# Pool mixing of a hybrid decoder layer: plain fp32 matmuls replaced by three fp32r matmuls of high and low parts

## The chip, the cores and the metric

The kernel runs on one core of one Trainium2 chip. Its five engines each work through a queue of their own: TensorE (PE in the profile; PEld is its weight load), VectorE (DVE), ScalarE (ACT), GpSimd (POOL) and SyncE (SP, which here only starts transfers). They wait for each other by semaphores. The metric is the device time of one execution, in microseconds (us); less is better.

## The reference

One decoder layer over 256 tokens of width 2048. A normalised input goes through one combined projection of twelve column groups of 512; three branches read it: causal attention of 8 heads, a pooling mixer of 4 groups of 128 channels, and cross-attention of 4 heads into 256 memory tokens. Each is gated, all are concatenated, projected out, added to the input and normalised. The change is in the pooling mixer:

```
outs = []
for g, w in enumerate(POOL_WINDOWS):                  # 2, 4, 8, 16
    csg = cs[..., g*128:(g+1)*128]                    # running sum of u
    prev = jnp.pad(csg, ((0, 0), (w, 0), (0, 0)))[:, :S]
    outs.append((csg - prev) / cnt)                   # trailing-window mean
pooled = jnp.stack(outs, axis=2) - uf                 # mean minus token
mixed = jnp.einsum('bsgc,gcd->bsgd', pooled, w_pool)  # four 128x128 maps
y_p = mixed * pool_scale * silu(g_p)
```

## The kernel before

The projections run in fp32r, which takes a matmul in one pass but keeps fewer bits than fp32. So every operand X is split into a high part (a copy rounded to fp32r) and a low part (X minus the high part), and a product is made of high x high, high x low and low x high.

**Units.** The weights come in pieces of 128 x 1024 numbers (two slices of 128 rows by 512 columns). A group of 512 columns (MK, MV, Q0, ..., U, GA0, GA1, GP, QM, GM, then the output groups) is eight units, a = 0 to 7. For unit n, SP loads the piece, ACT writes its high part `w_hi` (L916), DVE its low part `w_lo` (L1167), and PE multiplies (L660 by the high part, 512 columns: high and low part of the activations side by side; L663 by the low part, 256 columns). Four units' halves fit (`SPLIT = 4`): in the code of step n ACT and DVE split unit n + 4. ACT may overwrite a half when PE has used the unit before it (`piece_used`); PE waits for the low part of its unit (`lo_done`).

**Order.** The order of each engine is that of the code: a loop over the units, in which the other work is put behind conditions such as `g == GP and a == 3`. Nothing overtakes on an engine. In a step, ACT and DVE first split unit n + 4 and then do most of the step's other work; PE first multiplies its unit. So DVE's step a is not tied in time to PE's step a; it can lie before or behind it.

**The pooling.** `window_sums` and `window_means` on DVE make `u_pad[:, :, PAD:]` (4 blocks of 128 channels x 256 tokens), the second of them in steps 3 and 4 of GA1 (L1370 to L1372), and count `pooled_ready` up to 4. The maps `wp` (128 x 4 x 128) are loaded early by SP. In group GP, behind its unit a = 5, PE waits for both and multiplies (L879). ACT, in its own step GP 5, waits for `mixed`, scales the four results (L1103) and hands them to the gate.

**What else is in group GP.** ACT and DVE also split the memory keys there (`mk_hi` L1081 in ACT's step 1, `mk_lo` in DVE's step 2) and the memory values (`mv_hi` L1084 in ACT's step 3, `mv_lo` in DVE's step 4; both low parts by the helper at L1341), finish the gate of the group before (DVE L1454 in step 1, behind POOL's product L611), and split it (ACT L1114 in step 1, DVE L1459 in step 2). Their users come much later, with the group GM.

At the start of the kernel PE runs eleven matmuls of ones (L807), which compute nothing that is used.

The lines of PE that the change replaces:

```
if g == GP and a == 5:
    pe.wait_ge(wp_landed, 16)
    pe.wait_ge(pooled_ready, NF)
    for i in range(NF):
        m = pe.matmul(ps[:, bank0(g + 1) + i, 0:S], wp[:, i, :], u_pad[:, i, PAD:], ...)
    m.then_inc(mixed, 1)
```

Of the kernel before, what the change touches and what calls it, by code (L numbers as in the profile page):

```python
# [22 lines left out]
F32R = mybir.dt.float32r  # L23
ALU = mybir.AluOpType
ACT = mybir.ActivationFunctionType
AX = mybir.AxisListType

P = 128
D = 2048
S = 256  # L30
# [4 lines left out]
NF = COLS // P  # L35
# [4 lines left out]
PAD = WINDOWS[-1] // 2  # L40
# [77 lines left out]
def build(nc, x, mem, x_t, mem_head, columns, w_in, w_mem_kv, w_pool, w_out, final_g, out):  # L118
    with ExitStack() as ctx:
        def sb(name, shape, dt=F32, stack=ctx):  # L120
            return stack.enter_context(nc.sbuf_tensor(name, shape, dt))

        def sem(name):
            return ctx.enter_context(nc.semaphore(name))
# [7 lines left out]
        early = ExitStack()  # L132
        xT = sb("xT", [P, KT, 2, S], F32R, early)
        early.close()
        early = ExitStack()
# [4 lines left out]
        early = ExitStack()  # L140
# [3 lines left out]
        early = ExitStack()  # L144
        sb("y_of_branches", [P, (KT - NF) * 2 * S], F32, early)
        u_pad = sb("u_pad", [P, NF, PAD + S], F32, early)
        early.close()
        early = ExitStack()
        mem_rows = sb("mem_rows", [P, TH, D], F32, early)
        early.close()  # L150
        early = ExitStack()
# [5 lines left out]
        early = ExitStack()  # L157
# [3 lines left out]
        early = ExitStack()  # L161
# [43 lines left out]
        sum_b = sb("sum_b", [P, NF, PAD + S], F32, early)  # L205
        early.close()
        early = ExitStack()
        xs_hi = sb("xs_hi", [P, BLOCKS, 4, TPP, P], F32R, early)
        xs_lo = sb("xs_lo", [P, BLOCKS, 4, TPP, P], F32R, early)
        early.close()  # L210
# [97 lines left out]
        u_ready = sem("u_ready")  # L308
        pads_zero = sem("pads_zero")
        pooled_ready = sem("pooled_ready")  # L310
        mixed = sem("mixed")
        gate_tanh = sem("gate_tanh")
        gate_att = sem("gate_att")
# [41 lines left out]
        def bank0(g):  # L355

            return BANK.get(g, 4 * (g % 2))
# [271 lines left out]
        def _(pe):  # L629
# [199 lines left out]
            for n in range(PAIR):  # L829
                g, a = unit(n)  # L830

                if n == K_PAIR:
                    pe.wait_ge(evacuated, Q0 + 1)
                if n == V_PAIR:
                    pe.wait_ge(evacuated, Q1 + 1)
                if in_pair(n):
                    unit_of_pair(n)
                    if n == K_TURNED:
                        turn_keys()
                    continue  # L840
                if a == 0 and g >= 2:
                    pe.wait_ge(evacuated, g - 1)
                if a == 0 and g == U:
                    pe.wait_ge(kT_ready, 2)
                if a == 0 and g - 1 in BRANCHES:
                    pe.wait_ge(att_ready, 2 * (BRANCHES.index(g - 1) + 1))
                if n < HIGH_FIRST:
                    high_parts_first(n)
                    continue
                if g == MK:  # L850
                    pe.wait_ge(mem_lo, TPP * (a + 1))
                if g == Q0:
                    pe.wait_ge(x_lo, a + 1)
                if g == OUT0 and a % 2 == 0:
                    pe.wait_ge(y_lo, a // 2 + 1)
                pe.wait_ge(lo_done, n + 1)
                if g == OUT0:
                    rows_are_tokens(n, yT).then_inc(piece_used, 1)
                elif g in TOKENS_ON_ROWS:
                    rows_are_tokens(n, memT if g == MV else xT).then_inc(piece_used, 1)  # L860
                else:
                    rows_are_features(n, memT if g == MK else xT)

                if g in JOBS:
                    if a == int(g == MEM_JOB):
                        pe.wait_ge(evacuated, g)
                        scores(g, 0)
                        scores(g, 1)
                    if a == 4 + int(g == GA0):
                        turn_probs(g, 0)  # L870
                        turn_probs(g, 1)
                    if a == 6:
                        weigh_values(g, 0)
                        weigh_values(g, 1)
                if g == GP and a == 5:
                    pe.wait_ge(wp_landed, 16)
                    pe.wait_ge(pooled_ready, NF)
                    for i in range(NF):
                        m = pe.matmul(ps[:, bank0(g + 1) + i, 0:S], wp[:, i, :], u_pad[:, i, PAD:], start=True, stop=True)  # L879
                    m.then_inc(mixed, 1)  # L880

            pe.wait_ge(evacuated, OUT0)
# [15 lines left out]
        def _(act):  # L898
# [124 lines left out]
            for n in range(PAIR):  # L1023
# [55 lines left out]
                if g == GP and a == 1:  # L1079
                    act.wait_ge(mk_scaled, 1)  # L1080
                    act.activation(mk_hi[:, :, :], mkT[:, :, :], ACT.Copy).then_inc(mk_hi_done, 1)  # L1081
                if g == GP and a == 3:
                    act.wait_ge(mv_scaled, 1)
                    act.activation(mv_hi[:, :, :], mv[:, :, :], ACT.Copy).then_inc(mv_hi_done, 1)  # L1084
# [70 lines left out]
        def _(dve):  # L1155
# [183 lines left out]
            def low(lo, whole, hi):  # L1339

                return dve.tensor_tensor(lo[:, :, :], whole[:, :, :], hi[:, :, :].bitcast(F32), ALU.subtract)  # L1341
# [41 lines left out]
            for n in range(PAIR):  # L1383
# [47 lines left out]
                if g == GP and a == 2:  # L1431
                    dve.wait_ge(mk_hi_done, 1)
                    low(mk_lo, mkT, mk_hi).then_inc(mk_split, 1)
                if g == GP and a == 4:
                    dve.wait_ge(mv_hi_done, 1)
                    low(mv_lo, mv, mv_hi).then_inc(mv_split, 1)
# [145 lines left out]
```

## Time and profile before

| | us |
|---|---|
| median of 3 runs | 428.13 |
| lowest and highest of them | 428.09, 428.76 |
| the profiled execution's own time | 428.26 |
| its span in the profile | 426.5 |
| PE busy | 417.3 |
| DVE busy | 313.6 |
| ACT busy | 249.5 |
| POOL busy | 43.4 |

The span runs from the first to the last instruction that the profile shows; 1.76 us of the execution's time lie around it. Busy times are sums over the whole span. A duration of a matmul in the profile includes the time it spends in PE's pipeline, in which the next ones are already running: the distance from one start to the next is what a matmul costs in a stream of them. The same holds, by less, for DVE and ACT.

### The profile page before, as it was taken

The numbers are of one execution on the slowest core, as the hardware profiler recorded it, in microseconds if no ns is written. First come the engines' busy times: TensorE is split into PE (matmuls) and PEld (weight loads), VectorE is DVE, ScalarE is ACT, GpSimd is POOL, SyncE is SP. The second block draws the span as 40 slices with busy tenths as digits, with TensorE's granted clock in tenths as the row PEclk, the third lists the DMA queues.
The fourth block names the chain that finished last, engine by engine and source line by source line (L and its number), as shares of the span: only waits on it lengthen the run. The fifth ranks groups of instructions, "written<-read, shape, count | busy, mean of one in ns | idle before, by whom it ended". The sixth has DMA issues, their size and how long they took to land.

```text
span 426.5 us, 5775 instructions
## 1 busy us (share of the span) xinstructions
PE 417.3 (98%) x2184; PEld 357.9 (84%) x2184; DVE 313.6 (74%) x342; ACT 249.5 (58%) x335; POOL 43.4 (10%) x68
## 2 busy tenths in 40 slices
PE   8999999999999999999999999999999999999993
PEld 7888888888888888888888888888899888888882
DVE  4876888477987896856566778887667488897853
ACT  6764785257665667368465444755565566665611
POOL 1000003101001000000000341401000301000160
PEclk9999999999999999999999999999999999999998
DMA  8999739999599378955398256565646999467023
GB/s 285 415 414 421 315 105 303 297 412 320 146 386 271 129 25 328 421 226 197 100 116 243 62 184 202 192 199 167 228 148 223 247 405 275 186 246 295 3 87 110
DMA packets 29115, 99.48 MB, mean 233 GB/s; under 512 B 3872, under 2 KB 4384, under 8 KB 28192
## 3 DMA queue, kind: packets, MB, share of 16 engines
q1 hardware_dynamic: 24912, 84.31, 57.3%
q0 software_dynamic: 1728, 6.29, 8.0%
q10 hardware_dynamic: 2448, 8.52, 5.3%
q8 instruction: 17, 0.28, 0.3%
q14 instruction: 10, 0.08, 0.0%
HBM read 97.01 MB, written 2.10 MB: 232 GB/s over the span
## 4 chain that ended last, share of the span: by engine, by line
PE 91%; issue 3%; DVE 3%; DMA 1%; ACT 1%; DVEq 0%; POOLq 0%; POOL 0%; ACTq 0%
PE ps L660 29%; PE ps L663 14%; PE ps L719 4%; PE ps L717 4%; PE ps L718 4%; PE ps L676 4%; PE ps L678 4%; PE ps L677 4%; PE ps L702 4%; PE ps L700 4%; PE ps L701 4%; PE ps L641 3%; PE ps L648 1%; DMA mem_raw<-in_mem_head 1%; DVE x_f L1178 1%
## 5 line engine op out<-in xcount | busy, mean ns | idle before, releaser
L1167 DVE TENSOR_TENSOR w_lo<-w_raw,w_hi 128x1024 fp32r<-128x1024 f32 x131 | 163.3, 1263 | 61.5 <-ACT w_hi L916 60.6
L916 ACT ACTIVATE w_hi<-w_raw 128x1024 fp32r<-128x1024 f32 x131 | 135.9, 1056 | 64.7 <-PE ps L663 27.7
L660 PE MATMUL ps<-xT,w_hi 128*128 128x512 f32 x512 | 161.7, 397 | 0.0
L663 PEld LDWEIGHTS ps<-xT,w_lo 128*128 128x128 f32 x512 | 96.2, 188 | 22.7
L663 PE MATMUL ps<-xT,w_lo 128*128 128x256 f32 x512 | 100.6, 278 | 0.0
L660 PEld LDWEIGHTS ps<-xT,w_hi 128*128 128x128 f32 x512 | 78.3, 189 | 0.3
L717 PE MATMUL ps<-w_hi,xT 128*128 128x512 f32 x64 | 24.9, 389 | 0.0
L718 PE MATMUL ps<-w_lo,xT 128*128 128x512 f32 x64 | 24.9, 389 | 0.0
L719 PE MATMUL ps<-w_hi,xT 128*128 128x512 f32 x64 | 24.9, 389 | 0.0
L916 ACT ACTIVATE w_hi<-x_f 128x1024 fp32r<-128x1024 f32 x14 | 14.8, 1059 | 15.5 <-PE ps L719 10.1
L1167 DVE TENSOR_TENSOR w_lo<-x_f,w_hi 128x1024 fp32r<-128x1024 f32 x14 | 17.1, 1224 | 6.4 <-ACT w_hi L916 6.3
L1058 ACT ACTIVATE part_b<-ps 128x1024 f32<-128x1024 f32 x9 | 9.2, 1024 | 15.1 <-PE ps L663 15.1
L676 PE MATMUL ps<-w_hi,yT 128*128 128x512 f32 x46 | 17.9, 389 | 0.0
L677 PE MATMUL ps<-w_lo,yT 128*128 128x512 f32 x46 | 17.9, 389 | 0.0
L678 PE MATMUL ps<-w_hi,yT 128*128 128x512 f32 x46 | 17.9, 389 | 0.0
L718 PEld LDWEIGHTS ps<-w_lo,xT 128*128 128x128 f32 x64 | 12.0, 188 | 2.5
L717 PEld LDWEIGHTS ps<-w_hi,xT 128*128 128x128 f32 x64 | 12.0, 188 | 2.5
L719 PEld LDWEIGHTS ps<-w_hi,xT 128*128 128x128 f32 x64 | 12.0, 188 | 2.5
L641 PE MATMUL ps<-memT,w_hi 128*128 128x512 f32 x48 | 13.2, 396 | 0.7 <-DVE memT L1265 0.7
L611 POOL TENSOR_TENSOR gate<-gate,att 128x1024 f32<-128x1024 f32 x4 | 9.6, 2411 | 37.3 <-ACT part_b L1109 37.3
L1114 ACT ACTIVATE yT<-gate 128x1024 fp32r<-128x1024 f32 x4 | 4.2, 1062 | 15.0 <-DVE gate L1454 15.0
L621 POOL TENSOR_TENSOR x_res<-x_res,fg 128x512 f32<-128x512 f32 x6 | 8.0, 1365 | 49.0 <-DVE w_lo L1167 49.0
(220 smaller groups left out, 699.3 us busy)
## 6 DMA issues: line engine op xcount, KB each, us to landing
w_raw<-in_w_in SPq DMA_DIRECT2D x92, 512.0 KB, 6.7
w_raw<-in_w_out SPq DMA_DIRECT2D x30, 512.0 KB, 5.0
w_raw<-in_w_mem_kv SPq DMA_DIRECT2D x13, 512.0 KB, 12.2
x_f<-in_w_in SPq DMA_DIRECT2D x6, 512.0 KB, 7.1
x_f<-in_w_in POOLq DMA_DIRECT2D x6, 512.0 KB, 9.4
x_t_raw<-in_x_t SPq DMA_DIRECT2D x8, 256.0 KB, 12.9
rows<-in_x ACTq DMA_DIRECT2D x2, 1024.0 KB, 10.1
mem_rows<-in_mem ACTq DMA_DIRECT2D x2, 1024.0 KB, 10.2
```

The lines of the kernel that those rows point to most:

```text
L641: pe.matmul(ps[:, bank0(MK) + f, :], hi[:, t, f * P:(f + 1) * P], memT[:, kt], start=(kt == 0), stop=False, skip_group_check=True)
L660: pe.matmul(ps[:, bank0(g) + f, :], hi[:, t, f * P:(f + 1) * P], moving[:, kt], start=(kt == 0), stop=(kt == KT - 1), skip_group_check=True)
L663: m = pe.matmul(ps[:, bank0(g) + f, 0:S], lo[:, t, f * P:(f + 1) * P], moving[:, kt, 0], start=False, stop=(kt == KT - 1), skip_group_chec ...
L676: pe.matmul(acc, stationary[:, kt, 0, tok], hi[:, t, :], start=(kt == 0), stop=False)
L677: pe.matmul(acc, stationary[:, kt, 0, tok], lo[:, t, :], start=False, stop=False)
L678: m = pe.matmul(acc, stationary[:, kt, 1, tok], hi[:, t, :], start=False, stop=(kt == last))
L700: pe.matmul(ps[:, bank, :], left[0], hi[:, t, :], start=not begun, stop=False, skip_group_check=True)
L717: pe.matmul(acc, rows[:, kt, 0, tok], hi[:, t, :], start=not begun, stop=False, skip_group_check=True)
L718: pe.matmul(acc, rows[:, kt, 0, tok], lo[:, t, :], start=False, stop=False, skip_group_check=True)
L719: m = pe.matmul(acc, rows[:, kt, 1, tok], hi[:, t, :], start=False, stop=end_of, skip_group_check=True)
L916: act.activation(halves_of(n)[0], whole_of(n), ACT.Copy).then_inc(hi_done, 1)
L1167: dve.tensor_tensor(lo, whole_of(n), hi.bitcast(F32), ALU.subtract).then_inc(lo_done, 1)
```

## The change

PE's wait in GP 5 is now for a new semaphore `pool_split` (two counts), and each of the four fp32 matmuls is three fp32r matmuls of the same output size, into the same place. ACT writes the high parts of the maps and of the pooled values in its step GP 2, and DVE the low parts in its step GP 3. The four new tensors lie in the place that `sum_a` and `sum_b` share with others; that place doesn't grow.

```
@@ tensors
+        pooled_hi = sb("pooled_hi", [P, NF, S], F32R, early)
+        pooled_lo = sb("pooled_lo", [P, NF, S], F32R, early)
+        wp_hi = sb("wp_hi", [P, NF, P], F32R, early)
+        wp_lo = sb("wp_lo", [P, NF, P], F32R, early)
@@ PE, group GP, behind unit 5
-                    pe.wait_ge(wp_landed, 16)
-                    pe.wait_ge(pooled_ready, NF)
+                    pe.wait_ge(pool_split, 2)
                     for i in range(NF):
-                        m = pe.matmul(ps[:, bank0(g + 1) + i, 0:S], wp[:, i, :], u_pad[:, i, PAD:], start=True, stop=True)
+                        acc = ps[:, bank0(g + 1) + i, 0:S]
+                        pe.matmul(acc, wp_hi[:, i, :], pooled_hi[:, i, :], start=True, stop=False)
+                        pe.matmul(acc, wp_hi[:, i, :], pooled_lo[:, i, :], start=False, stop=False)
+                        m = pe.matmul(acc, wp_lo[:, i, :], pooled_hi[:, i, :], start=False, stop=True)
                     m.then_inc(mixed, 1)
@@ ACT
+                if g == GP and a == 2:
+                    act.wait_ge(wp_landed, 16)
+                    act.wait_ge(pooled_ready, NF)
+                    act.activation(wp_hi[:, :, :], wp[:, :, :], ACT.Copy).then_inc(pool_hi_done, 1)
+                    act.activation(pooled_hi[:, :, :], u_pad[:, :, PAD:], ACT.Copy).then_inc(pool_hi_done, 1)
@@ DVE
+                if g == GP and a == 3:
+                    dve.wait_ge(pool_hi_done, 2)
+                    low(wp_lo, wp, wp_hi).then_inc(pool_split, 1)
+                    low(pooled_lo, u_pad[:, :, PAD:], pooled_hi).then_inc(pool_split, 1)
```

How the rows stand on the engines, from units GP 4 to GM 2. In DVE's queue before, from the low part of unit GP 6 on (the L1167 rows are, in this order, GP 6, then GP 7 and GM 0, then GM 1 and GM 2):

```order
L1167 TENSOR_TENSOR w_lo<-w_raw,w_hi 128x1024 [waits hi_done]
L1341 TENSOR_TENSOR mk_lo<-mkT,mk_hi 128x1024 [waits mk_hi_done]
L1459 TENSOR_TENSOR yT<-gate,yT 128x4x256 [waits y_hi]
L1167 TENSOR_TENSOR w_lo<-w_raw,w_hi 128x1024 [waits hi_done] x2
L1341 TENSOR_TENSOR mv_lo<-mv,mv_hi 128x1024 [waits mv_hi_done]
L1167 TENSOR_TENSOR w_lo<-w_raw,w_hi 128x1024 [waits hi_done] x2
```

The same place after the change (L1182 is what L1167 was, L1356 what L1341 was):

```order
L1182 TENSOR_TENSOR w_lo<-w_raw,w_hi 128x1024 [waits hi_done]
L1356 TENSOR_TENSOR mk_lo<-mkT,mk_hi 128x1024 [waits mk_hi_done]
L1478 TENSOR_TENSOR yT<-gate,yT 128x4x256 [waits y_hi]
L1182 TENSOR_TENSOR w_lo<-w_raw,w_hi 128x1024 [waits hi_done]
L1356 TENSOR_TENSOR wp_lo<-wp,wp_hi 128x512 [waits pool_hi_done]
L1356 TENSOR_TENSOR pooled_lo<-u_pad,pooled_hi 128x1024
L1182 TENSOR_TENSOR w_lo<-w_raw,w_hi 128x1024 [waits hi_done]
L1356 TENSOR_TENSOR mv_lo<-mv,mv_hi 128x1024 [waits mv_hi_done]
L1182 TENSOR_TENSOR w_lo<-w_raw,w_hi 128x1024 [waits hi_done] x2
```

The two new low parts stand between the low parts of units GP 7 and GM 0. In ACT's queue after the change, from the split of the gate on (L926 was L916; its rows are the high parts of units GP 6, GP 7, GM 0, GM 1):

```order
L1129 ACTIVATE yT<-gate 128x4x256 [waits y_ready]
L926 ACTIVATE w_hi<-w_raw 128x1024 [waits landed2,piece_used]
L1095 ACTIVATE wp_hi<-wp 128x512 [waits pooled_ready,wp_landed]
L1096 ACTIVATE pooled_hi<-u_pad 128x1024
L926 ACTIVATE w_hi<-w_raw 128x1024 [waits landed3,piece_used]
L1099 ACTIVATE mv_hi<-mv 128x1024 [waits mv_scaled]
L926 ACTIVATE w_hi<-w_raw 128x1024 [waits landed4,piece_used]
L926 ACTIVATE w_hi<-w_raw 128x1024 [waits landed5,piece_used]
L1118 ACTIVATE att<-ps,cols 128x256 [waits y_ready,mixed]
```

The two new high parts stand between those of units GP 6 and GP 7. Nothing else has moved on any engine.

## Rows read from the trace of the kernel before

**Rows 1.** The page: busy times with shares of the span, and the chain's shares.

```profile
PE 417.3 (98%) x2184; PEld 357.9 (84%) x2184; DVE 313.6 (74%) x342; ACT 249.5 (58%) x335; POOL 43.4 (10%) x68
...
PE 91%; issue 3%; DVE 3%; DMA 1%; ACT 1%; DVEq 0%; POOLq 0%; POOL 0%; ACTq 0%
```

**Rows 2.** All waits of PE (what, for what: us in total, times, longest).

```profile
PE ps L807 <- POOL ones L546: 1.0, 1, 1.0
PE ps L641 <- DVE memT L1265: 0.7, 1, 0.7
```

**Rows 3.** Timeline of PE at the pool's mixing (start us, length us).

```profile
274.85 0.40 PE L663 MATMUL ps<-xT,w_lo 128*128 128x256 f32 x2
275.08 1.89 PE L879 MATMUL ps<-u_pad,wp 128*128 128x256 f32 x8
```

**Rows 4.** The chain of waits, same place (start us, length us).

```profile
275.24 1.73 PE ps L879 x8
```

**Rows 5.** Timeline of DVE, the units of group GP ([idle before <- releaser]).

```profile
273.14 1.23 DVE L1167 TENSOR_TENSOR w_lo<-w_raw,w_hi 128x1024 fp32r<-128x1024 f32 x1 [2.08 <-ACT w_hi L916]
274.29 1.76 DVE L1341 TENSOR_TENSOR mk_lo<-mkT,mk_hi 128x1024 fp32r<-128x1024 f32 x1
275.98 1.21 DVE L1459 TENSOR_TENSOR yT<-gate,yT 128x1024 fp32r<-128x1024 f32 x1
277.11 2.35 DVE L1167 TENSOR_TENSOR w_lo<-w_raw,w_hi 128x1024 fp32r<-128x1024 f32 x2
279.38 1.21 DVE L1341 TENSOR_TENSOR mv_lo<-mv,mv_hi 128x1024 fp32r<-128x1024 f32 x1
```

**Rows 6.** Timeline of PE: scores with the memory, first of 24, and what follows the last.

```profile
310.24 0.28 PE L746 MATMUL ps<-mk_hi,qm_hi 128*128 128x256 f32 x1
...
313.11 0.63 PE L660 MATMUL ps<-xT,w_hi 128*128 128x512 f32 x2
```

**Rows 7.** Timeline of ACT, same stretch.

```profile
271.10 1.07 ACT L1114 ACTIVATE yT<-gate 128x1024 fp32r<-128x1024 f32 x1 [3.04 <-DVE gate L1454]
272.07 1.99 ACT L916 ACTIVATE w_hi<-w_raw 128x1024 fp32r<-128x1024 f32 x2
```

**Rows 8.** Splits of 128x512, by line (duration ns min/median/max).

```profile
L1255 DVE TENSOR_TENSOR w_lo<-w_raw,w_hi x3: 685/687/692, 5.7 to 10.0; 128x512 fp32r<-128x512 f32 x3
...
L922 ACT ACTIVATE w_hi<-w_raw x3: 612/617/632, 5.0 to 9.1; 128x512 fp32r<-128x512 f32 x3
```

**Rows 9.** Timeline: PE after its wait for DVE at the start.

```profile
5.27 0.48 DVE L1265 SCALAR_TENSOR_TENSOR memT<-mem_raw,memT 128x256 fp32r<-128x256 f32 x1 [5.27 <-ACT memT L941]
...
5.81 1.20 PE L641 MATMUL ps<-memT,w_hi 128*128 128x512 f32 x4 [0.69 <-DVE memT L1265]
...
7.32 1.09 PE L641 MATMUL ps<-memT,w_hi 128*128 128x512 f32 x4
```

**Rows 10.** Timeline of POOL around it.

```profile
273.37 1.61 POOL L601 TENSOR_TENSOR s_raw<-gate,s_raw 128x256 f32<-128x256 f32 x1
287.42 2.42 POOL L611 TENSOR_TENSOR gate<-gate,att 128x1024 f32<-128x1024 f32 x1 [12.45 <-ACT part_b L1109]
```

**Rows 11.** PE's last matmul; windows after it (the third number from the end: granted clock).

```profile
418.78 0.28 PE L733 MATMUL ps<-w_hi,yT 128*128 128x256 f32 x1
...
423.50:424.00 0.50, 0.00 (x0) 0.00 (x0) 0.00 (x0) 0.00 (x0) 0.00 (x0) 0.80 1.25 393
424.00:425.00 1.00, 0.00 (x0) 0.00 (x0) 0.00 (x0) 0.00 (x0) 0.00 (x0) 0.50 0.98 336
```

**Rows 12.** PE's first matmuls: by line, then the timeline of two short windows.

```profile
L807 PE MATMUL ps<-ones x22: 275/421/583, 1.0 to 4.8; 128*128 128x128 f32 x22
...
1.01 1.23 PE L807 MATMUL ps<-ones 128*128 128x128 f32 x4 [1.01 <-POOL ones L546]
...
4.29 0.83 PE L807 MATMUL ps<-ones 128*128 128x128 f32 x6
```

More of the change, by code:

```diff
@@ L207, in build @@
         early = ExitStack()
+        pooled_hi = sb("pooled_hi", [P, NF, S], F32R, early)
+        pooled_lo = sb("pooled_lo", [P, NF, S], F32R, early)
+        wp_hi = sb("wp_hi", [P, NF, P], F32R, early)
+        wp_lo = sb("wp_lo", [P, NF, P], F32R, early)
+        early.close()
+        early = ExitStack()
         xs_hi = sb("xs_hi", [P, BLOCKS, 4, TPP, P], F32R, early)
@@ L310, in build @@
         pooled_ready = sem("pooled_ready")
+        pool_hi_done = sem("pool_hi_done")
+        pool_split = sem("pool_split")
         mixed = sem("mixed")
```

## The prediction, as it was put on record

> **What bounds the kernel now.** Read the page's busy times first: PE is busy for 98% of the span, and the chain that ended last runs through PE for 91% of it [rows 1]. Then PE's waits: in the whole execution it waits twice, 1.0 and 0.7 us, both in the first 6 us [rows 2]. So PE is the bound everywhere, a time taken off its stream comes off the end, and a time for which PE is made to wait goes onto the end, as long as no later wait of PE is there to take it up; there is none. The other engines matter only where they come too late for PE.
>
> Then read the place of the change. The eight passes of the four fp32 matmuls start at 275.08, directly behind the last matmul of unit GP 5 [rows 3], and hold PE for 1.73 us on the chain, 0.216 each [rows 4]. PE doesn't wait for the pooled values there, since they are done long before: it waits for nothing.
>
> Last, read DVE's timeline beside it, since PE is to wait for DVE now. A unit takes PE about 2.8 us, and DVE's queue is a fixed order. While PE ends GP 5 at 275.08, DVE has just begun `mk_lo` (274.29), which belongs to its own step GP 2 [rows 5]. DVE prepares units four ahead, so PE isn't disturbed by that; but other work in DVE's step a = 3 isn't done when PE is at a = 3, it is done when DVE gets there. This offset between the steps of the two engines is what decides the change.
>
> **PE's own work, a gain.** Removed: eight passes, 1.73 us [rows 4]. Added: twelve fp32r matmuls of 128x256. The same shape with the same pattern of high and low parts stands in the scores with the memory: 24 of them take from 310.24 to 313.11, 0.1196 each [rows 6]. 12 x 0.1196 = 1.435 us. The gain is 0.29 us, 0.07% of the whole. The bound on the bad side is the fp32 pass of the old code, 0.216: 12 x 0.216 = 2.59, a loss of 0.86; I take the scores' row, since type, shape and pattern are those of the change.
>
> The Trainium skill ("TensorE: Matmul & The Clock Gate", Back-to-back issue gap) gives a warm matmul of N columns as N/2.4 + 2.5 ns. That is 109 ns for 256 columns, so 1.31 us and a gain of 0.42; the 119.6 ns of the rows decides.
>
> **ACT's new work, hidden.** `wp_hi` and `pooled_hi` come behind the high part of unit GP 6, the first of the two L916 rows at 272.07; the second, GP 7, would follow at about 273.02 [rows 7]. What they wait for is long there. `wp_hi` is 128x512, 0.62 us alone [rows 8], some 0.53 in a row of them; `pooled_hi` is as large as `w_hi`, 0.95 in a row. So both end near 274.6, and the high part of GP 7 ends near 275.6 in place of 274.1. DVE wants that one only at 277.11 [rows 5]; 1.5 us of slack remain. The high parts of GM 0 and GM 1 move by the same 1.5 us and are wanted by DVE after 280. Cost: nothing; without that slack it would be up to 1.5 us on DVE.
>
> **PE's new wait, the loss.** `pool_split` comes from DVE, in this order: low part of GP 6 at 273.14, `mk_lo` at 274.29, the gate's low part at 275.98, the low parts of GP 7 and GM 0 from 277.11 on [rows 5]. The change puts its two subtractions between these last two. Two of them take 2.35, one alone 1.21, so the second starts 1.14 behind the first, at 278.25: there `wp_lo` starts now. It is 128x512, 0.687 long [rows 8], of which about 0.08 overlaps the next, as with the others; `pooled_lo` starts at 278.86 and takes 1.21, like `mv_lo` of the same size [rows 5]: it ends at 280.07. At the start of the kernel PE begins 0.06 us after the end of the DVE row that it waited for (5.27 + 0.48 = 5.75, then 5.81) [rows 9]. So PE begins the mixing at 280.13 and not at 275.08: a stall of 5.05 us. The first matmuls after that earlier wait took 1.20 for four where the next four took 1.09 [rows 9]: 0.1 more for a pipeline that has run empty.
>
> What bounds this term: DVE's rows up to 278.25 are those of before, since nothing ahead of them changes. The two new subtractions could be slowed by POOL, as `mk_lo` looks slowed: 1.76 us, while POOL's L601 runs from 273.37 to 274.98. But POOL has no work from there to 287.42 [rows 10], so I take 1.21; at `mk_lo`'s rate it would be 0.55 more for `pooled_lo` and about 0.3 for `wp_lo`. On the good side, two more starts that overlap better could save 0.1 or 0.2.
>
> **Who else waits.** Behind PE's stalled mixing stand units GP 6, GP 7 and all the rest; nothing overtakes it. ACT goes on meanwhile up to its scaling of the result, which waits for PE, and DVE goes on to the low part of GM 1. When PE comes back they are further ahead of it than before, by the 1.8 us of new DVE work less than the whole stall, so they make PE wait nowhere behind it. The loads from memory are also at least as early relative to PE. No second cost; and no return either, since PE has no later wait to shorten [rows 2]. The tail of the kernel hangs on PE's last matmuls and shifts with them.
>
> **Sum.** +5.05 - 0.29 + 0.1 = +4.86 us. Against the profiled execution's 428.26 this gives 433.1; against the median of 428.13, 433.0. I say 433.1.
>
> **Rival 1: the clock falls in the stall.** PE stands still from 275.24, the end of its last matmul, to 280.13, 4.9 us; nowhere in the trace of before does it do so in the middle. What the clock does then is seen only at the end: the last matmul ends at 419.06, and the granted clock goes from 1.00 to 0.50 (2.4 to 1.2 GHz) in the window from 423.5, whose mean of 0.80 puts the fall at 423.8, 4.7 us after it [rows 11]. That is as long as the stall, so this one fall says neither yes nor no. The price can be read at the kernel's start: the first four passes over the ones take 1.23 in all, the last six 0.83, the single ones 0.583 and 0.275 [rows 12]. So starts are (1.23 - 0.583)/3 = 0.216 apart at first and (0.83 - 0.275)/5 = 0.111 at the end, a half clock and a full one. The 22 start from 1.01 to 4.8: 21 distances of which about 14 are slow, 3.0 us at the half clock, which lose 1.5 us. With that, 433.1 + 1.5 = 434.6; where half as much is lost, 433.9. The bound is a second stretch of that kind, 436.1, for which no row speaks.
>
> The same page of the Trainium skill (HAM oscillation) warns that idle gaps of PE between bursts bring the half clock back, and that each gap pays for it anew; by it this rival, at 434.6, would be the forecast. Rows of before can't decide it, as no such gap is in them.
>
> **Rival 2, on the other side: DVE is in time and the wait costs nothing.** Then the time is 428.26 - 0.29 = 428.0, the same as before within what can be measured. It decides at the point where `pooled_lo` ends before 275.08. DVE would have to be 5 us earlier in its queue. It did stand idle for 2.08 us before 273.14, waiting for ACT's high part of GP 6, and lost 0.55 in `mk_lo` [rows 5]; without both it would still be 2.4 us late, and the change touches neither. Up to a stall of 1.15 us the result would still be "the same". Against it: every row ahead in DVE's queue is there before as after.
>
> **Rival 3: part of the stall is given back.** If after the stall PE's stream ran denser, because it was slowed by something that comes early now, the time would be lower, say 431 to 432. Against it: units before and behind have the same length, and PE waits for nothing.
>
> **How the numbers follow.** About 0.2% (0.86 us) is what a measurement of this kernel can tell from no change. Chances: forecast with the full clock 0.50, 433.1; clock falls 0.42, 433.9 to 434.8; in time 0.03, 428.0; given back 0.03, 431.5; faster by over 0.2%, for which I see no mechanism, 0.02. The range has to hold the first two with their bounds: below, 433.1 less 0.2 of overlap, less 0.13 for the median and less 0.3 for what the starts of the rows leave open, 432.4; above, 434.6 with up to 0.85 of slowed subtractions, of which I leave in half, and a somewhat longer cold stretch, 435.5. Faster 0.02, the same 0.03, slower 0.95.
>
> **What would show it.** PE's waits show a third one, of some 5 us, for DVE's `pooled_lo`; the first new matmul starts near 280.1, the twelve take 1.4 us, the next unit's start is 4.9 us later than before, and everything behind it, PE's last matmul too, is later by the same. DVE's `wp_lo` starts at 278.2 to 278.3. If the clock falls, the granted clock of a window around 280 to 284 is below 1.00 and matmuls there stand twice as far apart. I am wrong if ACT's new work delays the low part of GP 7 beyond 277.11, if the new subtractions are much longer than 1.9 us together, or if PE is found to begin the mixing before DVE's queue has come to it.

## The result, and the profile after

The changed kernel takes 434.41 us (median of 4 runs, 433.88 to 434.70) where the kernel before takes 428.15 (4 runs, 428.09 to 428.76): 1.0139 times as long, 95% interval 1.0127 to 1.0152. It is slower by 6.3 us. Run again later, beside other kernels, it took 435.55 (5 runs, 434.57 to 435.96), 1.0164 (1.0150 to 1.0178). The profiled execution took 434.70, 6.44 more than that of before.

A word on names first: the group behind GP in the kernel's order is QM. The units that the part on the change and the prediction call GM 0, GM 1 and GM 2 are QM 0, QM 1 and QM 2. Only the name was wrong; the rows and the places meant are the right ones.

All waits of PE in the profile after (what, for what: us in total, times, longest), against the two of [rows 2]:

```profile
PE ps L887 <- DVE pooled_lo L1356: 4.6, 1, 4.6
PE ps L815 <- POOL ones L554: 1.0, 1, 1.0
```

There is one large new wait, and it is for `pooled_lo`. The timeline of PE at the mixing, against [rows 3] (columns: start us, length us; L668 and L671 are what L660 and L663 were):

```profile
275.36 0.40 PE L671 MATMUL ps<-xT,w_lo 128*128 128x256 f32 x2
280.35 0.58 PE L887 MATMUL ps<-pooled_hi,wp_hi 128*128 128x256 f32 x1 [4.59 <-DVE pooled_lo L1356]
280.73 0.41 PE L888 MATMUL ps<-pooled_lo,wp_hi 128*128 128x256 f32 x1
280.94 0.41 PE L889 MATMUL ps<-pooled_hi,wp_lo 128*128 128x256 f32 x1
...
283.07 0.80 PE L668 MATMUL ps<-xT,w_hi 128*128 128x512 f32 x2
283.71 0.40 PE L671 MATMUL ps<-xT,w_lo 128*128 128x256 f32 x2
283.95 0.62 PE L668 MATMUL ps<-xT,w_hi 128*128 128x512 f32 x2
```

Two of the L671 matmuls take 0.23 (275.08 less 274.85 in [rows 3]), so PE would have gone on at 275.59; it goes on at 280.35, a stall of 4.76 us. The profile gives 4.59, since it counts from the modelled end of the last matmul. And from there the new matmuls start 0.21 apart, not 0.12 as in [rows 6]. The granted clock says why (windows; the third number from the end):

```profile
280.00:280.50 0.50, 0.15 (x1) 0.15 (x1) 0.50 (x2) 0.00 (x0) 0.00 (x0) 0.53 0.53 180
283.00:284.00 1.00, 1.00 (x7) 0.88 (x6) 0.69 (x1) 0.69 (x2) 0.00 (x0) 0.78 0.91 336
```

A mean of 0.53 over the first half microsecond is a fall from 1.00 to 0.50 at 280.03, and 0.78 over the later one is a rise back at 283.44: 2.4 to 1.2 GHz and back, 3.4 us in all, of which PE works 3.1.

DVE's queue in the same stretch, against [rows 5] (L1182, L1356 and L1478 are what L1167, L1341 and L1459 were):

```profile
274.52 1.77 DVE L1356 TENSOR_TENSOR mk_lo<-mkT,mk_hi 128x1024 fp32r<-128x1024 f32 x1
276.21 1.21 DVE L1478 TENSOR_TENSOR yT<-gate,yT 128x1024 fp32r<-128x1024 f32 x1
277.34 1.21 DVE L1182 TENSOR_TENSOR w_lo<-w_raw,w_hi 128x1024 fp32r<-128x1024 f32 x1
278.48 0.68 DVE L1356 TENSOR_TENSOR wp_lo<-wp,wp_hi 128x512 fp32r<-128x512 f32 x1
279.08 1.21 DVE L1356 TENSOR_TENSOR pooled_lo<-u_pad,pooled_hi 128x1024 fp32r<-128x1024 f32 x1
```

DVE never pauses in it; the low parts are simply last in a line of five. The kernel's splits are at the places and of the lengths that the prediction gave, 0.23 us later, as the rows ahead of them are in this execution.

### The profile page after: what moved, and what is told of

Its sections match the earlier page's. It is cut to its first block, busy times and chain, and to the rows that moved or that the text cites. A ratio compares the mean times of both kernels' runs of the same rounds, so it can differ in the third digit from the quotient of the medians.

```text
span 432.9 us, 5787 instructions
## 1 busy us (share of the span) xinstructions
PE 419.8 (97%) x2188; PEld 360.5 (83%) x2188; DVE 315.3 (73%) x344; ACT 251.1 (58%) x337; POOL 43.4 (10%) x68
## 4 chain that ended last, share of the span: by engine, by line
PE 87%; DVE 6%; issue 3%; ACT 1%; POOL 0%; DVEq 0%; POOLq 0%; ACTq 0%
PE ps L668 26%; PE ps L671 13%; PE ps L727 4%; PE ps L725 4%; PE ps L726 4%; PE ps L684 4%; PE ps L686 4%; PE ps L685 4%; PE ps L710 4%; PE ps L709 4%; PE ps L708 4%; PE ps L649 3%; DVE w_lo L1182 2%; PE ps L656 1%; ACT w_hi L926 1%
## 5 line engine op out<-in xcount | busy, mean ns | idle before, releaser
L1182 DVE TENSOR_TENSOR w_lo<-w_raw,w_hi 128x1024 fp32r<-128x1024 f32 x131 | 163.4, 1262 | 65.2 <-ACT w_hi L926 64.4
L926 ACT ACTIVATE w_hi<-w_raw 128x1024 fp32r<-128x1024 f32 x131 | 136.0, 1056 | 65.0 <-PE ps L671 27.4
L668 PE MATMUL ps<-xT,w_hi 128*128 128x512 f32 x512 | 161.8, 397 | 0.0
L671 PEld LDWEIGHTS ps<-xT,w_lo 128*128 128x128 f32 x512 | 96.2, 188 | 22.6
L671 PE MATMUL ps<-xT,w_lo 128*128 128x256 f32 x512 | 100.6, 278 | 0.0
L668 PEld LDWEIGHTS ps<-xT,w_hi 128*128 128x128 f32 x512 | 78.5, 189 | 0.3
L926 ACT ACTIVATE w_hi<-x_f 128x1024 fp32r<-128x1024 f32 x14 | 14.8, 1059 | 15.7 <-PE ps L727 10.1
L1182 DVE TENSOR_TENSOR w_lo<-x_f,w_hi 128x1024 fp32r<-128x1024 f32 x14 | 17.1, 1223 | 6.8 <-ACT w_hi L926 6.7
```

Source lines behind the costliest of these rows:

```text
L668: pe.matmul(ps[:, bank0(g) + f, :], hi[:, t, f * P:(f + 1) * P], moving[:, kt], start=(kt == 0), stop=(kt == KT - 1), skip_group_check=True)
L671: m = pe.matmul(ps[:, bank0(g) + f, 0:S], lo[:, t, f * P:(f + 1) * P], moving[:, kt, 0], start=False, stop=(kt == KT - 1), skip_group_chec ...
L926: act.activation(halves_of(n)[0], whole_of(n), ACT.Copy).then_inc(hi_done, 1)
L1182: dve.tensor_tensor(lo, whole_of(n), hi.bitcast(F32), ALU.subtract).then_inc(lo_done, 1)
```

## The experiments

Three questions were open: whether the loss is the wait or the added work, what the clock's share is, and whether the gain on PE is real. The table has every further kernel that was run; `before` is the median of the kernel before on the same chip. "Stall" is from the moment at which PE would have gone on to the first matmul of the mixing, in the one profiled execution. The rows with the same number under `before` were run together on one chip, the others on other chips.

| kernel | median us | lowest, highest | before | ratio, 95% interval | stall |
|---|---|---|---|---|---|
| fit | 428.25 | 427.81, 428.81 | 428.22 | 0.9997 (0.9988, 1.0006) | 0 |
| fit_fp32 | 428.32 | 427.99, 429.02 | 428.22 | 1.0003 (0.9994, 1.0012) | 0 |
| warm | 432.95 | 432.48, 433.12 | 428.22 | 1.0109 (1.0093, 1.0124) | 4.48, filled |
| wait_only | 435.22 | 434.30, 436.89 | 428.22 | 1.0153 (1.0137, 1.0169) | 4.63 |
| stall1 | 429.44 | 429.03, 429.94 | 428.26 | 1.0026 (1.0016, 1.0035) | 1.60 |
| stall2 | 430.87 | 430.11, 431.82 | 428.26 | 1.0049 (1.0030, 1.0068) | 2.77 |
| stall3 | 433.40 | 432.10, 433.93 | 428.26 | 1.0104 (1.0083, 1.0125) | 3.86 |
| fit2 | 427.92 | 427.51, 428.55 | 428.26 | 0.9987 (0.9979, 0.9996) | 0 |
| splits_only | 428.37 | 427.95, 428.76 | 428.28 | 1.0000 (0.9990, 1.0009) | 0 |
| after_fp32 | 435.67 | 433.04, 437.42 | 428.28 | 1.0163 (1.0124, 1.0202) | 5.13 |
| after_again | 435.55 | 434.57, 435.96 | 428.28 | 1.0164 (1.0150, 1.0178) | 5.13 |
| fit2_fp32 | 428.58 | 428.14, 429.06 | 428.28 | 1.0006 (0.9996, 1.0015) | 0 |

### wait_only: the wait without the work

```
@@ before.py, PE, group GP, behind unit 5
                     pe.wait_ge(pooled_ready, NF)
+                    pe.wait_ge(lo_done, n + 4)
```

> The kernel before with one wait more and nothing else: at the mixing PE also waits for DVE's low part of the third unit ahead (the first of group QM), which ends at 279.46 in the trace of before. No splits, plain fp32 matmuls. Theory (the wait on DVE's queue is the loss): a stall of 4.4 us, 432.6 to 432.8 with the full clock, 434.2 to 434.6 if it falls (then eight fp32 passes run at the half clock too). Rival (the loss is ACT's and DVE's added work or the new matmuls): 428.2.

A single line turns 428.2 into 435.2. Not one instruction is added to ACT or DVE, and the matmuls are the old ones. PE's waits and its timeline:

```profile
PE ps L880 <- DVE w_lo L1168: 4.5, 1, 4.5
...
275.90 0.40 PE L663 MATMUL ps<-xT,w_lo 128*128 128x256 f32 x2
280.76 3.75 PE L880 MATMUL ps<-u_pad,wp 128*128 128x256 f32 x8 [4.46 <-DVE w_lo L1168]
283.95 1.41 PE L660 MATMUL ps<-xT,w_hi 128*128 128x512 f32 x2
...
286.83 0.63 PE L660 MATMUL ps<-xT,w_hi 128*128 128x512 f32 x2
```

So the wait is the loss: it ties PE to a place in DVE's queue that PE had passed without harm until then. The time came out above both values that were expected. In this execution (436.89, the highest of four) the clock stayed low for 6.8 us, from 279.94 to 286.76:

```profile
279.50:280.00 0.50, 0.00 (x0) 0.00 (x0) 0.50 (x1) 0.00 (x0) 0.00 (x0) 0.94 0.00 0
...
286.00:287.00 1.00, 1.00 (x5) 0.89 (x4) 0.00 (x0) 0.12 (x1) 0.00 (x0) 0.62 0.23 86
```

From the first pass of the mixing to the third pair of L660 it takes 6.07 us (280.76 to 286.83), where the kernel before needs 3.12: the clock, with the restart of PE's pipeline, cost 2.95 us here, twice what the prediction had allowed. The rest of this execution's loss is the stall of 4.63 us and 1.05 us that it had lost before it came to the mixing (its last matmul ahead of the wait starts at 275.90, where before has 274.85); 0.34 us of that is a wait for a low part at 92.81 that before doesn't have.

### splits_only: the work without the wait

```
@@ after.py, PE, group GP, behind unit 5
-                    pe.wait_ge(pool_split, 2)
+                    pe.wait_ge(wp_landed, 16)
+                    pe.wait_ge(pooled_ready, NF)
...
-                        pe.matmul(acc, wp_hi[:, i, :], pooled_hi[:, i, :], start=True, stop=False)
-                        pe.matmul(acc, wp_hi[:, i, :], pooled_lo[:, i, :], start=False, stop=False)
-                        m = pe.matmul(acc, wp_lo[:, i, :], pooled_hi[:, i, :], start=False, stop=True)
+                        m = pe.matmul(acc, wp[:, i, :], u_pad[:, i, PAD:], start=True, stop=True)
```

> The kernel before with the changed kernel's four splits on ACT and DVE in their places, and nobody who waits for them: PE waits for the pooled values as before and does four plain fp32 matmuls. Theory (the added work of ACT and DVE is hidden, only PE's wait for it costs): 428.2 to 428.4, the same as before. Rival (1.5 us more on ACT and 1.7 us more on DVE make PE wait for its units later): 429 or more, with a wait of PE for w_lo.

428.37 against 428.28, ratio 1.0000. ACT's 1.5 us and DVE's 1.7 us of added work cost nothing where they stand; no wait of PE for `w_lo` appears. Its trace also shows the distance that decides: PE's mixing starts at 275.32, DVE's `pooled_lo` at 278.54.

```profile
275.32 1.89 PE L888 MATMUL ps<-u_pad,wp 128*128 128x256 f32 x8
...
278.54 1.21 DVE L1355 TENSOR_TENSOR pooled_lo<-u_pad,pooled_hi 128x1024 fp32r<-128x1024 f32 x1
```

### warm: the stall without the idling

```
@@ after.py, PE, group GP, behind unit 5
+                    keep_warm(20, bank0(g + 1))
                     pe.wait_ge(pool_split, 2)
```

> The changed kernel with twenty matmuls of ones (results unused) on PE ahead of its wait, which fill 4.3 us of the 5 us in which it stood still; splits and wait are as in the changed kernel. Theory (stall 4.8 to 5.0 us, and a half clock behind it that costs 1.5 us): the clock stays at 1.00, PE goes on at the same moment as before, the twelve matmuls stand 0.12 apart: 433.0, 1.4 less than the changed kernel. Rival (the clock's part of the loss is nothing, or the new matmuls are slow by themselves): 434.4 and matmuls 0.21 apart. If twenty matmuls run past the end of DVE's low part they cost PE what is over, some tenths at most.

432.95, as expected, and 1.46 below the changed kernel's 434.41 (2.6 below its second series, after_again). The matmuls of ones fill the stall, the granted clock stays at 1.00, and what follows stands 0.12 apart, but for the first, which takes 0.22:

```profile
278.00:279.00 1.00, 1.00 (x11) 1.00 (x11) 1.00 (x2) 0.00 (x0) 0.00 (x0) 1.00 0.09 12
...
275.02 4.63 PE L815 MATMUL ps<-ones 128*128 128x128 f32 x40
279.50 0.39 PE L888 MATMUL ps<-pooled_hi,wp_hi 128*128 128x256 f32 x1
279.72 0.28 PE L889 MATMUL ps<-pooled_lo,wp_hi 128*128 128x256 f32 x1
279.84 0.28 PE L890 MATMUL ps<-pooled_hi,wp_lo 128*128 128x256 f32 x1
```

PE works longer and the kernel is faster. The clock's share of the loss is thereby measured, and apart from the stall. The two traces give it without the spread of the medians: from the first matmul of the mixing to the second pair of L668 warm takes 279.50 to 281.74, 2.24 us, and the changed kernel 280.35 to 283.95, 3.60; the clock's share is 1.36.

### stall1, stall2, stall3: the low parts earlier in DVE's queue

```
@@ after.py, DVE, the four lines of the low parts (all three kernels)
-                if g == GP and a == 3:
-                    dve.wait_ge(pool_hi_done, 2)
-                    low(wp_lo, wp, wp_hi).then_inc(pool_split, 1)
-                    low(pooled_lo, u_pad[:, :, PAD:], pooled_hi).then_inc(pool_split, 1)
@@ stall1
+                if g == GP and a == 2:
+                    dve.wait_ge(pool_hi_done, 2)
+                    low(wp_lo, wp, wp_hi).then_inc(pool_split, 1)
+                    low(pooled_lo, u_pad[:, :, PAD:], pooled_hi).then_inc(pool_split, 1)
                 if g == GP and a == 2:
                     dve.wait_ge(mk_hi_done, 1)
                     low(mk_lo, mkT, mk_hi).then_inc(mk_split, 1)
```

In stall2 the same four lines stand directly behind `mk_lo`, in stall3 directly behind the gate's low part (L1459 of before), so ahead of the low part of GP 7; in the changed kernel they are behind that too.

> The changed kernel with its two low parts one place earlier in DVE's queue: between the low part of unit GP 6 and mk_lo. Nothing else. Theory (the stall is the end of pooled_lo less the end of PE's unit GP 5): the high parts are there at 274.8, the subtractions end at 276.7 to 277.2 (POOL works beside them), a stall of 1.6 to 2.1 us, too short for the clock to fall: 429.6 to 430.2. Rival (the wait itself or the fp32r form costs the time, wherever the subtractions stand): 433 or more.

> As stall1, but with the low parts behind mk_lo. They end at 277.8 in the times of the trace of before: a stall of 2.8 us. Theory: 430.7 to 431.1 if the clock holds. Clock theory: below the changed kernel's stall by far, so the clock should hold in all or nearly all executions; should it fall, 1.5 or more above.

> As stall1, but with the low parts behind the gate's low part, just ahead of the low part of unit GP 7. They end at 278.9: a stall of 3.9 us, 1.1 less than in the changed kernel. Theory: 431.9 to 432.2 while the clock holds; executions in which it falls are 1.5 us (or, after wait_only, 3 us) above these. I expect it to fall in fewer executions than in the changed kernel, so a median near 432.0 and a wider spread upward.

Each place in the queue costs about its length: stalls of 1.60, 2.77, 3.86 and 4.76 us, each from one execution, where one subtraction in a row stands 1.14 behind the other. The times follow, 1.2, 2.6, 5.1 and 6.3 above before. The first two are a little less than their stalls, as PE's gain of 0.28 (shown below) is in them; what is over the stall in the other two is the clock. In stall1 it fell in none of ten executions, as far as their mean granted clocks tell: 0.994 to 0.998, as in before (0.994 to 0.997). In stall2 three executions have 0.997 and take 430.1 to 431.0; the fourth, the profiled one, has 0.993 and takes 431.82. In stall3 all four have 0.990 to 0.993, where the expectation had the clock fall in fewer of them; so its median is 433.40 and not near 432.0.

Stall2's trace shows a fall that I had not thought possible after so short a pause. PE's last matmul before the stall ends at 275.0, and the clock is down at 277.0, 2.0 us later:

```profile
274.60 0.40 PE L671 MATMUL ps<-xT,w_lo 128*128 128x256 f32 x2
277.60 0.58 PE L887 MATMUL ps<-pooled_hi,wp_hi 128*128 128x256 f32 x1 [2.60 <-DVE pooled_lo L1356]
277.98 0.42 PE L888 MATMUL ps<-pooled_lo,wp_hi 128*128 128x256 f32 x1
...
276.50:277.00 0.50, 0.00 (x0) 0.00 (x0) 0.50 (x1) 0.50 (x1) 0.00 (x0) 1.00 0.60 238
277.00:277.50 0.50, 0.00 (x0) 0.00 (x0) 0.50 (x2) 0.50 (x2) 0.00 (x0) 0.51 0.00 0
```

In stall3 it falls behind the stall, when PE has worked again for 0.6 us: the granted clock is 1.00 up to 280.0 and 0.50 from there. PE is back at 279.39; its fourth and fifth matmuls start 0.12 apart, the sixth 0.17 and the seventh 0.22 behind the one before it:

```profile
279.39 0.39 PE L887 MATMUL ps<-pooled_hi,wp_hi 128*128 128x256 f32 x1 [3.69 <-DVE pooled_lo L1356]
...
279.84 0.28 PE L887 MATMUL ps<-pooled_hi,wp_hi 128*128 128x256 f32 x1
279.96 0.38 PE L888 MATMUL ps<-pooled_lo,wp_hi 128*128 128x256 f32 x1
280.13 0.42 PE L889 MATMUL ps<-pooled_hi,wp_lo 128*128 128x256 f32 x1
280.35 0.42 PE L887 MATMUL ps<-pooled_hi,wp_hi 128*128 128x256 f32 x1
```

### after_again and after_fp32: the same stall, and how long the clock stays low

after_fp32 keeps the changed kernel's splits and wait and takes back only the form of the matmuls:

```
@@ after.py, PE
-                        pe.matmul(acc, wp_hi[:, i, :], pooled_hi[:, i, :], start=True, stop=False)
-                        pe.matmul(acc, wp_hi[:, i, :], pooled_lo[:, i, :], start=False, stop=False)
-                        m = pe.matmul(acc, wp_lo[:, i, :], pooled_hi[:, i, :], start=False, stop=True)
+                        m = pe.matmul(acc, wp[:, i, :], u_pad[:, i, PAD:], start=True, stop=True)
```

> The changed kernel once more, unchanged, beside the others on one chip. Theory: stall 4.8 to 5.0 us; the clock falls in nearly every execution, since it fell in most of those of the shorter stall of stall3 (median 433.4 there): median 434.2 to 434.6, single executions between 433.8 and 434.8, and if it holds in one of them that one is near 433.0.

> The changed kernel with its splits and its wait, but the mixing as four plain fp32 matmuls. The stall is the same, 4.8 to 5.0 us. Theory at the full clock: 0.29 us more than the changed kernel. With the half clock behind the stall, as it was there in wait_only: 435 to 437, where the clock stays low for 3.4 us in some executions and 6.8 in others; if the kind of matmul behind the stall has nothing to do with that, 434.7 to 435.2 like the changed kernel.

The second series of the changed kernel missed its expectation: 435.55, 1.1 more than the first. Its profiled execution has the clock low from about 278.5 to 285.3 (the windows' means give both points), 6.8 us like wait_only, and this with the fp32r matmuls:

```profile
278.00:279.00 1.00, 0.00 (x0) 0.00 (x0) 1.00 (x2) 0.62 (x1) 0.00 (x0) 0.76 0.00 0
284.00:286.00 2.00, 2.00 (x10) 1.72 (x9) 0.00 (x0) 0.90 (x3) 0.00 (x0) 0.67 0.64 215
...
275.01 0.39 PE L671 MATMUL ps<-xT,w_lo 128*128 128x256 f32 x2
280.37 0.58 PE L887 MATMUL ps<-pooled_hi,wp_hi 128*128 128x256 f32 x1 [4.96 <-DVE pooled_lo L1356]
...
283.09 1.05 PE L668 MATMUL ps<-xT,w_hi 128*128 128x512 f32 x2
```

So the long stretch isn't bound to plain fp32 matmuls, which had been my thought after wait_only; the rival of after_fp32 (that the kind of matmul has nothing to do with it) stands better. The profiled execution of after_fp32 has 6.8 us too (from 278.8 to 285.6). The mean clock of an execution goes with the length: 0.993 in after's profiled one with its 3.4 us, 0.986 in the three with 6.8 us. Both come with both kinds of matmul: after, wait_only and after_fp32 each have two executions at 0.986 and two at 0.992 or 0.993. after_fp32 itself ranges from 433.04 to 437.42 in four executions and can't tell 0.3 us. What decides between 3.4 and 6.8 us isn't settled by these runs. PE is cold at work for 5.0 us of the 6.8 in after_again, where it was for 3.1 in the first profile, and its fourth pair of L668 starts 5.85 us behind the first matmul of the mixing (280.37 to 286.22) and not 4.99 (280.35 to 285.34): 0.86 us more. But a mean clock of 0.986 doesn't always go with a longer time: the two such executions of the first series took 434.35 and 434.47, less than its profiled one. So the 1.1 us between the two series' medians isn't explained by the clock alone; the profiled execution of the second also had the longer stall, 5.13 for 4.76.

### fit and fit_fp32: the same work at a place where nobody has to wait

```
@@ after.py, ACT: the four lines of the high parts
-                if g == GP and a == 2:
+                if g == GP and a == 1:
@@ DVE: the low parts, behind the gate (then L1454) in step GP 1
-                if g == GP and a == 3:
+                if g == GP and a == 1:
```

fit_fp32 is the same with four plain fp32 matmuls behind the wait.

> The changed kernel with the same work in another place: the two high parts on ACT in its step GP 1 (where ACT stood idle for 3.0 us), the two low parts on DVE in its step GP 1 behind the gate (where DVE stood idle for 2.1 us). Theory (the loss is the place in DVE's queue, and the clock that falls in the stall): no wait of PE at the mixing, no fall of the clock, 0.29 us gained on PE: 427.8 to 428.1 against 428.15 before, so 6.4 us less than the changed kernel. Rival (the splits themselves or the fp32r matmuls cost several us wherever they stand): 430 or more.

> As fit, with the splits done and waited for, but the mixing itself as four plain fp32 matmuls as before; the difference to fit is PE's own gain alone. Theory: eight passes of 0.216 against twelve of 0.120, 0.29 us more than fit, so 428.1 to 428.4, no difference to before. Rival (the fp32r form gains nothing in the stream): equal to fit within 0.1 us. Rival (the splits cost time): above 428.6.

The stall and the fall of the clock are gone: 428.25, 6.2 us less than the changed kernel with the same instructions. That settles the place. But fit is no faster than before, where 427.8 to 428.1 was expected, and only 0.07 faster than fit_fp32, which by the times alone is what the rival said (the fp32r form gains nothing). On PE's stream the gain is there: from the first matmul of the mixing to the second pair of L668, fit takes 275.21 to 277.35, 2.14 us; fit_fp32 takes 275.17 to 277.59, 2.42. It is given back three microseconds later:

```profile
279.20 0.40 PE L671 MATMUL ps<-xT,w_lo 128*128 128x256 f32 x2
279.84 0.73 PE L668 MATMUL ps<-xT,w_hi 128*128 128x512 f32 x2 [0.24 <-DVE w_lo L1182]
```

PE is at unit GP 7 at 279.43 and gets its low part at 279.79. fit_fp32 comes there at 279.68 and finds it ready (279.66), so it loses nothing. DVE is late for it, since four of its subtractions in a row take 1.76 in place of 1.21, and POOL's take 1.72 in place of 0.74 (the timelines of both engines):

```profile
271.83 1.76 DVE L1356 TENSOR_TENSOR pooled_lo<-u_pad,pooled_hi 128x1024 fp32r<-128x1024 f32 x1
273.52 1.76 DVE L1182 TENSOR_TENSOR w_lo<-w_raw,w_hi 128x1024 fp32r<-128x1024 f32 x1
275.20 1.77 DVE L1356 TENSOR_TENSOR mk_lo<-mkT,mk_hi 128x1024 fp32r<-128x1024 f32 x1
276.89 1.76 DVE L1474 TENSOR_TENSOR yT<-gate,yT 128x1024 fp32r<-128x1024 f32 x1
...
272.47 1.72 POOL L605 TENSOR_TENSOR s_raw<-gate 128x256 f32<-128x256 f32 x1
274.16 1.72 POOL L607 TENSOR_TENSOR s_raw<-s_raw,gate 128x256 f32<-128x256 f32 x1
```

In these rows DVE works without a pause beside POOL, and the starts on both engines are 1.7 us apart: each holds up the other at every instruction. The Trainium skill ("SBUF — State Buffer", SBUF: two separate sides) states that the two engines share a port pair and that, for a DVE instruction with two inputs in SBUF against one of POOL that reads SBUF, the first to start blocks the other for its whole length; the trace agrees: POOL's 0.74 has become about a DVE instruction and its own time.

### fit2 and fit2_fp32: and what isn't urgent out of the way

```
@@ fit.py, DVE: mk_lo
-                if g == GP and a == 2:
+                if g == QM and a == 4:
```

> As fit, and mk_lo (which nobody wants before group GM) is moved on DVE from its step GP 2 to QM 4. In fit DVE and POOL held each other up from 271.4 on and PE waited 0.4 us for the low part of unit GP 7, which ate the 0.28 us that the mixing gained. Theory: with one subtraction less ahead of it that wait goes, and the 0.28 us stays: 427.9, 0.3 less than before and fit (within the spread of single executions, so only as a mean). Rival (another wait of that kind comes up): equal to before.

> As fit2, but the mixing as four plain fp32 matmuls. Theory: PE's own gain is 0.28 us and nothing eats it in fit2 (427.92 there), so 428.2, no difference to before. Rival (fit2 is faster by the moved mk_lo, not by the matmuls): 427.9.

fit2 is the fastest of all: 427.92 in 12 runs, 0.9987 of before (0.9979 to 0.9996), so 0.3 us less, and PE waits for no low part. fit2_fp32 takes 428.58 in 11 runs, where 428.2 was expected; it isn't faster than before, so the rival, that moving `mk_lo` was the gain, falls. The two differ by 0.66 us, more than the 0.28 that PE's stream shows. They ran on different chips, and the intervals of their ratios to before just meet; I read no more from it than the sign.

## Why the prediction was right

The forecast was 433.1 with a range of 432.4 to 435.5; measured were 434.41 and, in the second series, 435.55, just above the range. The sign and the main cause, the stall, were right; of the two likeliest cases the second one came, a stall with a fall of the clock. The number 433.1 itself was reached by no execution of the changed kernel (the lowest took 433.88): the range held the first series because it had been drawn wide enough for that second case.

- **PE's gain, 0.29 forecast.** 0.28 on PE's stream (2.42 to 2.14, fit_fp32 and fit). The row of the scores [rows 6] was the right one: the twelve matmuls of fit start 0.120 apart. The 0.109 from the formula of the Trainium skill ("TensorE: Matmul & The Clock Gate", Back-to-back issue gap) was too low here as well.
- **ACT's work hidden.** In the profile after, the high parts run from 273.25 to 274.81, and DVE's low part of GP 7 doesn't wait. splits_only shows it for both engines: nothing.
- **The stall, 5.05 forecast.** 4.76 in the profile after and 5.13 in after_again. Every row of the sum came as given: `wp_lo` 0.68, `pooled_lo` 1.21, PE 0.06 behind its end (279.08 + 1.21 = 280.29, then 280.35). What moved was the distance between the engines ahead of the change: in the profile after, PE was 0.51 us later than in that of before and DVE 0.23. It is a matter of the single execution: the first four long matmuls take 1.72 there and 1.20 in [rows 9], and at 28.8 us, where before is at 28.3 in its stream, the 0.51 us is there. 1.72 for four is the spacing of the half clock for some of them, though the granted clock of the profile reads 1.00 there, as it does over the slow passes of ones in [rows 12].
- **The empty pipeline, 0.1 forecast.** 0.10: where PE starts again at the full clock, in warm and in stall1, the first matmul of the mixing takes 0.22 and the next ones 0.12.
- **No second cost, no return.** PE waits nowhere behind the mixing, and its scores with the memory start 6.5 us later (316.7 for 310.2 in [rows 6]), as the end does (432.9 for 426.5): what is lost at the mixing is neither raised nor lowered until the end.
- **The clock.** This is where the forecast chose wrongly: it gave 0.50 to the clock that holds and 0.42 to the fall. The fall came in all nine executions of the changed kernel, going by their mean clocks (0.986 to 0.993, where before has 0.994 to 0.997); the two profiled ones show it. The warning of the Trainium skill ("TensorE: Matmul & The Clock Gate", HAM oscillation), by which the fall was the forecast, was right. 434.6, the time of this rival, is 0.2 above the first series and 0.95 below the second. The step that failed: I set the stall against the one fall that the trace showed, 4.7 us after the last matmul [rows 11], and called it undecided. One such distance isn't the least distance; stall2 shows 2.0.
- **The clock's price, 1.5 forecast.** Between the first matmul of the mixing and the second pair of L668 the profile after takes 280.35 to 283.95, 3.60 us, and fit 2.14: 1.46, of which 0.10 is the empty pipeline and 1.36 the clock. The median of warm lies 1.46 below the first series' and 2.6 below the second's. The row of the start [rows 12] gave a fair price by some luck: it shows 3.0 us of slow passes, and PE happened to work cold for 3.1 in this execution. Where PE worked cold for longer it cost more: 5.0 us of it in after_again made 2.32 (5.85 to the fourth pair of L668, where fit takes 3.53). So the forecast's price holds only for the short stretch. The prediction called a second cold stretch something "for which no row speaks", and it came in wait_only, after_again and after_fp32.

The account of the profiled execution: 0.51 from the start, 4.76 of stall, 1.46 of clock and empty pipeline, less 0.28, is 6.45; its time rose by 6.44. The same for after_again: 0.16, 5.13, and 2.32 less 0.28, is 7.33; its time, 435.57, is 7.31 above the 428.26 of before.

The other rivals: DVE was not in time, and nothing was given back. The first is possible if the work is moved, as fit shows, but not by this change.

## What to carry to other kernels

Where two engines work through fixed orders, compare them by their times in the trace and not by the step they are in: a result written "two steps earlier" in the code may come 5 us after the engine that wants it. Before a wait is added to the engine that bounds the kernel, look where the producer's queue stands at that moment, and put the producing work into its idle time ahead of it. A stall on TensorE costs more than its length once the clock falls, here by 1.4 us and more. Matmuls that nobody uses were cheaper than silence here (warm, 432.95 for 434.41), and an earlier place for the work was cheaper than both (fit, 428.25).

## What the runs showed of the hardware that I had not expected

- A pause of PE of 2.8 us was enough once in four executions to halve its clock; the fall came 2.0 us after the last matmul. In other executions it came 3.1 (after_again), 3.6 (wait_only, after_fp32), 4.3 (after) and 4.7 [rows 11] after it. In stall3 it came 0.6 us after PE had begun again. In ten executions with a pause of 1.6 us it didn't come.
- The clock stayed low for 3.4 us in some profiled executions (after, stall2, stall3) and for 6.8 in others (wait_only, after_again, after_fp32), with PE at work for most of it in all of them (2.8 of the 3.4 us in stall2, 6.0 of the 6.8 in wait_only). What decides is open.
- In fit, DVE and POOL held each other up in turns over some 6 us, 1.21 becoming 1.76 on the one and 0.74 becoming 1.72 on the other. Filling an idle gap of DVE wasn't free while POOL worked beside it.
- The granted clock of the profile reads 1.00 over the first 5 us, though the passes of ones stand 0.216 apart there at first and 0.111 at the end [rows 12].
